# A two-layer transformer kernel on one NeuronCore: the first projection in two passes, x transposed by products with a diagonal

## What is computed

```python
mod = silu(c) @ w_ada + b_ada                      # c: one row of 1024; w_ada: 1024 x 6144
shift1, scale1, gate1, shift2, scale2, gate2 = split(mod, 6)
h = rms_norm(x, norm1_g) * (1 + scale1) + shift1   # x: 512 x 1024
z = h @ w_in                                       # 1024 x 2112, in five pieces
c_q, c_kv, k_pe, dq, dk, dv = split(z)
...
```

## Time and profile before

| | us |
|---|---|
| median of 3 runs | 2017.85 (2015.47 to 2018.05) |
| the profiled execution's own time | 2011.72 |
| its span in the trace | 2009.9 |
| c's first product starts | 39.00 |
| c's last product ends | 68.23 |
| expert weights' stage | about 485 to 854 |

### The profile page before, as it was taken

One profiled execution on the slowest core, in us unless ns is written; L12 is line 12 of the kernel. 1 busy time (PEld: TensorE's weight loads), 2 busy tenths in 40 slices (PEclk: granted clock), 3 DMA queues, 4 the chain that ended last, 5 costly groups with the idle time before them and its releaser, 6 DMA issues.

```text
span 2009.9 us, 22143 instructions
## 1 busy us (share of the span) xinstructions
PE 1893.5 (94%) x8716; PEld 1220.1 (61%) x8716; DVE 762.4 (38%) x1551; ACT 612.0 (30%) x1111; POOL 628.7 (31%) x374
## 2 busy tenths in 40 slices
PE   5999999999989989989999999899899999999998
PEld 3554337634333333368887868544577678888786
DVE  6552266523222222262899225366340220000002
ACT  3112562311011011062223344466343342232212
POOL 0000432011011010054443325555434235555532
PEclk9999999999999999999999999999999999999999
DMA  9452003889999999963224321110142023322321
GB/s 383 168 211 87 32 22 131 316 359 426 428 427 427 428 428 428 396 217 111 84 84 126 105 84 67 49 33 22 64 157 84 1 95 101 109 84 88 122 84 63
DMA packets 90037, 358.29 MB, mean 178 GB/s; under 512 B 6955, under 2 KB 35883, under 8 KB 75484
## 3 DMA queue, kind: packets, MB, share of 16 engines
q1 hardware_dynamic: 87088, 351.75, 45.1%
q0 software_dynamic: 2304, 4.20, 0.6%
q10 hardware_dynamic: 556, 1.13, 0.1%
HBM read 355.42 MB, written 5.83 MB: 180 GB/s over the span
## 4 chain that ended last, share of the span: by engine, by line
PE 75%; DMA 13%; DVE 5%; ACT 3%; issue 2%; POOL 1%; SPq 0%; POOLq 0%; DVEq 0%; ACTq 0%
PE bank L754 14%; PE bank L756 14%; PE bank L755 14%; PE bank L729 11%; DMA slots<-in_w_expert_gate 9%; PE bank L1160 7%; DMA slots<-in_w_expert_up 3%; PE bank L1373 2%; PE bank L1393 2%; PE bank L881 1%; PE bank L1362 1%; PE bank L1131 1%; PE bank L1185 1%; ACT area L1983 1%; DMA slots<-in_w_ada 1%
## 5 line engine op out<-in xcount | busy, mean ns | idle before, releaser
L2815 POOL TENSOR_TENSOR low_r<-slots,high_r 128x2048 fp32r<-128x2048 f32 x82 | 380.0, 4634 | 511.1 <-ACT high_r L1612 511.1
L755 PE MATMUL bank<-xl_r,high_r 128*128 128x512 f32 (+1 forms) x832 | 320.3, 385 | 0.0
L754 PE MATMUL bank<-area_r,high_r 128*128 128x512 f32 x800 | 312.7, 391 | 0.0
L756 PE MATMUL bank<-area_r,low_r 128*128 128x512 f32 x800 | 311.3, 389 | 0.0
L1612 ACT ACTIVATE high_r<-slots 128x2048 fp32r<-128x2048 f32 x82 | 156.9, 1914 | 402.9 <-PE bank L756 402.1
L1160 PE MATMUL bank<-slots,area 128*64 128x512 f32 x992 | 226.8, 601 | 22.5 <-DMA slots<-in_w_expert_gate 16.2
L755 PEld LDWEIGHTS bank<-xl_r,high_r 128*128 128x128 f32 x832 | 156.3, 188 | 31.6 <-issue 0.5
L756 PEld LDWEIGHTS bank<-area_r,low_r 128*128 128x128 f32 x800 | 150.2, 188 | 31.5
L754 PEld LDWEIGHTS bank<-area_r,high_r 128*128 128x128 f32 x800 | 150.2, 188 | 31.4 <-issue 0.6
L1160 PEld LDWEIGHTS bank<-slots,area 128*64 128x64 f32 x992 | 67.5, 137 | 165.4 <-issue 126.0
L2616 DVE SCALAR_TENSOR_TENSOR bank<-area,cols,bank 128x512 f32<-128x512 f32 x232 | 153.4, 747 | 0.0
(11 more groups left out here) (423 smaller groups left out, 2811.7 us busy)
## 6 DMA issues: line engine op xcount, KB each, us to landing
slots<-in_w_expert_down SPq DMA_DIRECT2D x32, 2048.0 KB, 16.3
slots<-in_w_expert_up SPq DMA_DIRECT2D x32, 2048.0 KB, 16.2
slots<-in_w_expert_gate SPq DMA_DIRECT2D x30, 2048.0 KB, 15.0
slots<-in_w_in SPq DMA_DIRECT2D x15, 2048.0 KB, 7.9
slots<-in_w_ada SPq DMA_DIRECT2D x11, 2048.0 KB, 12.0
slots<-in_ffn_in_w SPq DMA_DIRECT2D x22, 1024.0 KB, 6.7
slots<-in_ffn_out_w SPq DMA_DIRECT2D x5, 2048.0 KB, 7.8
slots<-in_w_out SPq DMA_DIRECT2D x4, 2048.0 KB, 8.1
```

What stands on the lines that cost most here:

```text
L754: nc.tensor.matmul(out, xh, yh, start=start and n == 0, stop=False)
L755: nc.tensor.matmul(out, xh, yl, start=False, stop=False)
L756: last = nc.tensor.matmul(out, xl, yh, start=False, stop=stop and n == len(pairs) - 1)
L2815: nc.gpsimd.tensor_tensor(low_half(m), raw_half(m), high_half(m), ALU.subtract).then_inc(s["w_low"], 1)
```

## The change

The first projection is split by input features: a first pass over feature tiles 0 to 3 of all four token tiles, a second over 4 to 7. The parts of the modulation are taken in the order 0, 2, 1, 3, so that shift and scale of the first half of the features come first; DVE's new function `modulate(half)` keeps two sets of columns, finishes half of `A1` and changes four tiles of `hT`, and stands once after parts 0 and 2 and once after 1 and 3. `ada_columns` 1 and 3 write into banks 4 and 5 and stand inside the first pass. c's weights come in two halves.

x is no longer scaled by ACT and put through transpose mode: ACT writes four diagonal matrices of 128x128 (identity times 1/rms of a token tile, `DIAG1`), and PE multiplies x as it is by them, 32 ordinary products of 128 columns. 36 products of ones with ones stand at PE's start and 22 after the toep products. The toep copies go from ACT to DVE, ahead of the variance. All DVE modulation parts stand behind the variance.

SP loads x first, then parts 0, 2, half of c's weights, 1, 3, the rest; parts wait for DVE's use of the slot and not for PE; a table `FIRST_SLOTS` says which chunk has which slot. The first half of w_out is issued ahead of the `up` weights. Semaphores with one use each are put together (`asked_of_act`, `given_by_act`).

```diff
-plan("toep", ["act"] * 3)
+plan("toep", ["dve"] * 3)
...
+ADA_ORDER = (0, 2, 1, 3, 4, 5, 6, 7, 8, 9, 10, 11)
+ADA_PLACE = {j: n for n, j in enumerate(ADA_ORDER)}
+FIRST_SLOTS = (0, 1, 3, 0, 2, 1, 3, 0, 1, 3, 2, 0, 3, 2, 2, 3, 1, 1)
+ADA_CHUNK = {0: 0, 2: 1, 1: 2, 3: 3, 4: 5, 5: 6, 6: 9, 7: 10, 8: 12, 9: 13, 10: 15, 11: 16}
...
-        XN1 = E(4096, 4096, TT)
+        SQUARES1 = A(8192, 4096, TT)
+        DIAG1 = E(0, 512, TT)
...
+        def columns_bank(j):
+
+            return banks[2 + ADA_PLACE[j]] if j in (1, 3) else None
...
-                if 0 <= prev < 4:
-                    sp.wait_ge(s["ada_acc"], prev + 1)
+                if prev in ADA_CHUNK.values():
+                    sp.wait_ge(s["ada_acc"], [ADA_CHUNK[j] for j in ADA_ORDER].index(prev) + 1)
...
-            sp.wait_ge(s["xpose_full"], KT)
...
-            ada(1)
+            ada(4, 5)
             chunk(CHUNK_NO["kpe"], [(0, w_in[:, :, 512:576])])
             chunk(CHUNK_NO["dq"], [(0, w_in[:, :, 576:1088])])
-            ada(2)
+            ada(6, 7)
             chunk(CHUNK_NO["dk"], [(0, w_in[:, :, 1088:1600])])
-            ada(3)
+            ada(8, 9, 11, 10)
             chunk(CHUNK_NO["dv"], [(0, w_in[:, :, 1600:2112])])
-            ada(4)
+            chunk(CHUNK_NO["wo"], [(0, w_out[:, :, 0:C])])
             chunk(CHUNK_NO["up"], [(0, w3(io["w_q_up"][0])), (2 * 768, w3(io["w_kv_up"][0]))])
...
+            def ones_products(n):
+
+                for _ in range(n):
+                    nc.tensor.matmul(banks[7][:, 0:P], ones[:, :], ones[:, :], start=True, stop=True)
+
+            pe.wait_ge(s["ones_set"], 1)
+            ones_products(36)
...
+            ones_products(22)
+            pe.wait_ge(s["xn_ready"], TT)
+            for c in range(KT):
+                n = XP["norm1"] + c
+                if n >= 2:
+                    pe.wait_ge(xpose_emptied[n % 2], n // 2)
+                for t in range(TT):
+                    last = nc.tensor.matmul(banks[6 + n % 2][:, t * P:(t + 1) * P], X[:, t, c * P:(c + 1) * P], DIAG1[:, t, :],
+                                            start=True, stop=True)
+                last.then_inc(s["xpose_full"], 1)
             ada_columns(0)
-            ada_columns(1)
-            norm_transposes("norm1", XN1)
-            for j in range(2, 4):
-                ada_columns(j)
+            ada_columns(2)
...
+            c_product(0, 0)
+            c_product(1, 0)
+            ada_columns(1)
+            c_product(2, 0)
+            c_product(3, 0)
+            ada_columns(3)
+            loaded(CHUNK_NO["c"])
+            for t in range(TT):
+                c_product(t, 1)
...
-            norm(XN1)
-            for n in range(3):
-                width = C if n < 2 else NG - 2 * C
-                bank = full(FIRST["toep"] + n)
-                empty(nc.scalar.activation(BROW[0:NH, n * C:n * C + width], bank[0:NH, 0:width], ACT.Copy))
...
+            norm(SQUARES1)
             act.wait_ge(s["norm1_ready"], 1)
             for t in range(TT):
-                nc.scalar.activation(XN1[:, t, :], X[:, t, :], ACT.Copy, scale=rstd[:, t:t + 1]).then_inc(s["xn_ready"], 1)
+                nc.scalar.activation(DIAG1[:, t, :], ID, ACT.Copy, scale=rstd[:, t:t + 1]).then_inc(s["xn_ready"], 1)
...
-            ada_part(0, 0)
...
+            for n in range(3):
+                width = C if n < 2 else NG - 2 * C
+                bank = full(FIRST["toep"] + n)
+                nc.vector.tensor_copy(BROW[0:NH, n * C:n * C + width], bank[0:NH, 0:width]).then_inc(s["dve_emptied"], 1)
...
+            def modulate(half):
+
+                piece = slice(4 * half, 4 * half + 4)
+                keep_columns(half)
+                keep_columns(2 + half)
+                dve.wait_ge(s["dve_emptied"], emptied("dve", ADA_GROUP[2 + half]))
+                then(nc.vector.scalar_tensor_tensor(A1[:, piece], A1[:, piece], 1.0, cols[:, V_N1 + 4 * half:V_N1 + 4 * half + 4],
+                                                    ALU.add, ALU.mult))
+                for c in range(4 * half, 4 * half + 4):
+                    dve.wait_ge(xpose_emptied[c % 2], c // 2 + 1)
+                    nc.vector.tensor_scalar(hT[:, c, :], hT[:, c, :], A1[:, c:c + 1], B1[:, c:c + 1], ALU.mult, ALU.add
+                                            ).then_inc(s["h_ready"], 1)
+
+            dve.wait_ge(s["given_by_act"], GIVEN["csil"])
+            ada_part(0, first_rstd)
+            ada_part(2)
+            modulate(0)
+            ada_part(1)
+            ada_part(3)
+            modulate(1)
             ada(1)
```

More of the change, by code:

```diff
@@ L882, in _ @@
                                             stop=k == KT - 1)
-                last.then_inc(s["proj_done"], 1)
+                if half:
+                    last.then_inc(s["proj_done"], 1)
+            pe.wait_ge(s["c_half"], 16)
+            pe.wait_ge(s["dve_emptied"], emptied("dve", ADA_GROUP[2]))
+            c_product(0, 0)
[7 more added lines that the diff above has]
+                c_product(t, 1)
+            transposed_emptied(XP["norm1"] + KT)
             ada(1)
@@ L1334, in _ @@
             split_emptied("mix")
-            pe.wait_ge(s["cmp_bias_loaded"], 64)
+            pe.wait_ge(s["extras_loaded"], 128)
             for h in range(NH):
@@ L1547, in _ @@
             act.wait_ge(s["cols_loaded"], 32)
-            nc.scalar.activation(csil, cols[:, V_C:V_C + KT], ACT.Silu).then_inc(s["csil_ready"], 1)
+            nc.scalar.activation(csil, cols[:, V_C:V_C + KT], ACT.Silu).then_inc(s["given_by_act"], 1)
             def transposed(n):
@@ L1653, in _ @@
                 empty(last)
-            act.wait_ge(s["latent_var"], 1)
-            nc.scalar.activation(stdc, varc, ACT.Sqrt).then_inc(s["latent_std"], 1)
+            act.wait_ge(s["asked_of_act"], ASKED["latents"])
+            nc.scalar.activation(stdc, varc, ACT.Sqrt).then_inc(s["given_by_act"], 1)
             ada(1)
@@ L1927, in _ @@
                     split_weights(FIRST_HALF["gc1"] + 2)
-            act.wait_ge(s["ln_var_ready"], 1)
-            nc.scalar.activation(RSQ, RSQ, ACT.Sqrt).then_inc(s["ln_std_ready"], 1)
+            act.wait_ge(s["asked_of_act"], ASKED["layer_norm"])
+            nc.scalar.activation(RSQ, RSQ, ACT.Sqrt).then_inc(s["given_by_act"], 1)
             for c in range(KT):
@@ L2180, in ada @@
                 for n, j in enumerate(ADA_PARTS[part]):
-                    ada_part(CHUNK_NO[f"ada{part}"] + n, j)
+                    ada_part(j)
             ropes = [0]
@@ L2205, in _, with keep_columns @@
             nc.vector.memset(ones[:], 1.0).then_inc(s["ones_set"], 1)
-            dve.wait_ge(s["csil_ready"], 1)
-            ada_part(0, 0)
+            def keep_columns(j):
+                columns = full(ADA_GROUP[j])
+                if columns_bank(j) is not None:
+                    columns = columns_bank(j)
+                at = 4 * j if j < 4 else 16 + 4 * (j - 6)
+                nc.vector.tensor_tensor(small[:, at:at + 4],
+                                        columns[:, 0:256].rearrange("p (n c) -> p n c", c=64)[:, :, 0:1]
+                                        .rearrange("p n c -> p (n c)"),
+                                        cols[:, V_BA + at:V_BA + at + 4], ALU.add).then_inc(s["dve_emptied"], 1)
+            for n in range(3):
+                width = C if n < 2 else NG - 2 * C
+                bank = full(FIRST["toep"] + n)
+                nc.vector.tensor_copy(BROW[0:NH, n * C:n * C + width], bank[0:NH, 0:width]).then_inc(s["dve_emptied"], 1)
             norms[0] += 1
```

136 lines of the change are left out of this document (62 added, 74 removed).

## The result

The changed kernel took 2002.74 us (median of 5 runs, 2001.58 to 2007.27) beside 2015.47 for the kernel before (2013.28 to 2018.05): a ratio of 0.9942, 95% interval 0.9925 to 0.996. The ratio goes by means and stands for 11.7 us less, with 8 to 15 as the interval; the two medians are 12.7 apart. The profiled execution of after has a span of 2000.9 us and took 2002.74 itself; that of before 2009.9 and 2011.72. In the two traces the change is therefore worth 9.0 us. Of the 9.9 us between forecast and time, 2.4 are that median, which stands at 2015.47 with five runs; the other 7.5 are gain that was not forecast.

What follows compares the result with a forecast made beforehand. PE was taken to bound the kernel, with DVE's modulation and the x path meeting before the projection; its end moves from 68.23 to 62.8, 5.4 less, taken as 5.2: 2017.85 to 2012.65 us, range 2009.0 to 2018.0.

Steps and rivals of the forecast that it cites:

- What bounds, and that the shift is carried: Whole kernel: PE has 75% of the chain; the opening's shift reaches the end one to one, expert weights stage included.
- the first term of the sum: Start of DVE's chain: ACT's bias scaling ends at 12.86 and comes last, squares follow, variance at 17.2.
- It can land earlier too; then the gain is up to 1 us more: Late-transfer rival (chance 0.10), its other direction: the 2 KB table lands early, up to 1 us more gain.
- by about 9: Opening: x, now the first transfer, is there by about 9, since the first 2 MB took 8.1 us to land.
- Durations: Opening and projection: diagonal products 8.0 us, columns 0.95 each, waits 1.13, projection 27.5 plus 3.0 for two passes.
- Clock: Projection: the clock stays at 2.4 GHz, saving the 1.7 us that its fall cost before.
- The rival that it falls at a wait: Clock falls at one or both waits of 1.1 us, 1.7 each: 2014.4 or 2016.1; chance 0.25.
- Ones products: PE's start: 36 end at 12.6, toep and 22 more at 20.0, bringing full clock before diagonal products at 21.3.
- Behind the opening: After the projection: only the opening is costed, its shift carried to the end; 5.2 for small losses at semaphores.

Runs made afterwards that it cites:

- better: Changed kernel with the reciprocal one step earlier on DVE and `ada_columns(3)` after the first product of tile 3: 2003.59 us, ratio 0.9945.
- the first pair: Traces of before and changed kernel from the main measurement, spans 9.0 us apart; the second pair repeats both unaltered (2015.36 and 2004.2 us), spans 9.2 apart.

## Why the prediction was wrong in size

**What bounds, and that the shift is carried.** Right. The lead of the projection's end, 7.5 us, was there unchanged at 290 and, but for the step by chance near 294, at 850: the expert stage moved along.

**The failed step is the first term of the sum**, "What then comes last is ACT's bias scaling, which ends at 12.86". Its cause, the table's landing, was taken at before's time although the change exchanges the transfers beside it; the text saw this ("It can land earlier too; then the gain is up to 1 us more") and bounded it at 1. It landed 2.4 earlier, and the two swaps of x and part 0 show that this comes from which transfer SP issues first. The bound was wrong too. Two other things in the forecast were off, and they set where the gain ends: x was there at 10.5 and not "by about 9", and the weights of DVE's first part landed at 15.4, where the forecast had no wait for them; that wait cost 0.4 us. So variance 14.91 for 17.2, first product 29.60 for 32.3. The term was mis-sized by 2.3 us at the variance, and 2.1 us of it reached the projection's end (60.70 for 62.8).

**Durations.** Right within 0.5 us: diagonal products 7.59 (8.0 forecast, by the row of 64 columns), columns 1.90, wait 1.12, second pass's wait 1.42 (1.13), passes at 0.44 us a record (0.43, which is 0.5 us over 64). Reciprocal to products 1.53 (1.8). DVE was ahead of PE at columns 1, by 0.2 to 0.3 us (0.2 forecast), and at columns 3. From the first product to the projection's end went 31.1 us, 30.5 by the forecast.

**Clock.** Right in what it did: 1.00 from 20 to 61 in both traces, 1.7 us won back. The rival that it falls at a wait was a real one: it happened in `better`, at the same wait of 1.12 us, so part of this hit is luck. What holds the clock up isn't the absence of transposes: it fell with the diagonal products in before, and stood at 1.00 with the transposes back in the changed kernel.

**Ones products.** Right: the last of them end at 18.5 (20.0 forecast), before the diagonal products are due at 19.15, and they are worth 2.3 us.

**Behind the opening** there was no term ("I therefore cost the opening alone"), and this is the second step that failed. In the pairs of traces 1.2 us came at the last load. The load took 6.1 and 6.2 us in the two traces of before, 5.7 in before with x first, and 4.8 to 5.0 in the eleven others, before with ones or diagonal products among them. It goes with the program, not with two passes. The traces hold one thing that goes with it: a transfer of instructions, 16 KB, on a queue of its own. In the three traces with the long load it begins 1.2 to 2.7 us after that load's issue. In the eleven others it begins at least 3.1 us before the issue, or 4.3 us and more after it, when the load is nearly through. The transfer in before, in the window 1968.8 to 1975.0 (count, MB, share):

```profile
q8 instruction: 1, 0.02, 1.5%
```

That it is the cause isn't shown: no run moves this transfer alone.

**The account.** 5.4 forecast, and 2.1 from the early start less small losses, are the 7.5 of the first pair (7.3 in the second). The 1.2 of the last load comes to it. With the steps by chance taken out, the first pair leaves 8.9 us and the second 8.1; these are estimates from the leads. The ratios stand for 11.7 and 10.9 us, with intervals that begin at 8.1 and 7.7, and the mean spans are 10.7 apart. Some 2 us of that are in no step that the traces show as steady; whether they are the chance of the clock or something steady stays open. For the forecast it means: with the early table and the last load in it, the same sum gives about 2009.3, just inside its range. The median of before is another 2.4, and some 4 us of the 9.9, which go by medians of five executions, stay unexplained.

## What to carry to other kernels

When a change puts another transfer at the head of a queue, time anew every small load that shares the DMA engines, in both directions: here the forecast hung on a wait for 2 KB, and it was 2.4 us off. Starting inputs early pays only with a consumer that can start on part of them; here early x, the diagonals and half of the loads gave nothing in one pass, and 7.3 to 7.5 us with two. And where one execution differs from another by several stretches of low clock, read a gain stage by stage in two traces of each kernel before crediting it.

## What the runs showed of the hardware

- A 2 KB table issued from ACT's queue was there for ACT at 12.4 to 12.6 us with a 2 MB weight transfer at the head of SP's queue, and at 9.8 to 10.4 with x there, in the kernel before and in the changed one alike.
- A full fp32 product of 128x128 by 128 columns, two records, took 0.237 us (7.59 / 32) at full clock and 0.31 (9.90 / 32) where it began at the lower one.
- The clock fell to 0.50 behind a wait of 1.12 us in one program and not in another with the same wait; such falls cost 1.6 to 2.2 us each where PE is busy, and recur at the same places of the program without coming in each execution (near 294 in both traces of before, and at that place in one of two of after). With transposes running, it rose from 0.50 to 1.00 at 27.2 in the changed kernel with transposes back.
- The same 1 MB transfer at the same place of the program took 5.7 to 6.2 us in three traces and 4.8 to 5.0 in eleven; in the three, and in no other, a 16 KB transfer of instructions began 1.2 to 2.7 us after its issue.
